# A decoder trunk on one core: the last down projection as seven block products instead of eight

## The reference

```python
def swiglu_ffn(h, w_gu, w_down):
    g, u = jnp.split(h @ w_gu, 2, axis=-1)
    return (jax.nn.silu(g) * u) @ w_down
...
for i in range(DEPTH):                     # DEPTH = 2
    x = x + 0.5 * swiglu_ffn(rmsnorm(x, n_ffn1[i]), ffn1_w_gu[i], ffn1_w_down[i])
    ...                                    # token mixer, cross attention
    x = x + 0.5 * swiglu_ffn(rmsnorm(x, n_ffn2[i]), ffn2_w_gu[i], ffn2_w_down[i])
return rmsnorm(x, n_final)
```

## Time and profile before

| | us |
|---|---|
| median of 3 runs | 1934.61 |
| lowest, highest | 1934.22, 1935.02 |
| the profiled execution, whole time | 1933.99 |
| its span in the trace | 1932.2 |
| PE busy | 1923.7 |
| DVE busy | 1347.7 |
| ACT busy | 964.4 |
| POOL busy | 329.0 |

### The profile page before, as it was taken

The page is one execution under the profiler, slowest core; times in us unless marked ns, Lnnn a source line. Parts: engine busy times, 40 slices in busy tenths (PEclk is TensorE's granted clock), DMA queues, the critical chain, the costliest instruction groups (busy, mean ns, idle before and its releaser), DMA issues.

```text
span 1932.2 us, 31908 instructions
## 1 busy us (share of the span) xinstructions
PE 1923.7 (100%) x12020; PEld 1740.5 (90%) x12020; DVE 1347.7 (70%) x2111; ACT 964.4 (50%) x1612; POOL 329.0 (17%) x331
## 2 busy tenths in 40 slices
PE   9999999999999999999999999999999999999998
PEld 7998998888898889989998998999898889989997
DVE  7865875687765658847866985687487569837854
ACT  7542554355554546524544653365356446524543
POOL 2200212100112121101201120121312123401200
PEclk9999999999999999999999999999999999999999
DMA  6734974323443627736943683695353427847932
GB/s 181 164 109 117 181 153 138 109 67 108 131 128 114 173 87 171 157 103 150 186 111 119 135 169 98 140 189 132 110 179 121 109 70 180 173 153 164 188 109 87
DMA packets 385097, 263.82 MB, mean 137 GB/s; under 512 B 19314, under 2 KB 367600, under 8 KB 384992
## 3 DMA queue, kind: packets, MB, share of 16 engines
q1 hardware_dynamic: 303840, 209.22, 36.4%
q0 software_dynamic: 72224, 51.19, 17.3%
q10 hardware_dynamic: 8928, 2.11, 0.5%
HBM read 251.99 MB, written 10.49 MB: 136 GB/s over the span
## 4 chain that ended last, share of the span: by engine, by line
PE 97%; DVE 1%; issue 1%; ACT 1%; DMA 0%; ACTq 0%
PE ps L434 19%; PE ps L435 18%; PE ps L436 18%; PE ps L1068 14%; PE ps L1067 14%; PE ps L1066 14%; DVE w_lo L2118 0%; ACT w_hi L1447 0%; PE ps L992 0%; PE ps L926 0%; DVE sums L2876 0%; DMA x_tok<-in_x 0%; DVE sums L2896 0%; DVE up L3065 0%; PE ps L1192 0%
## 5 line engine op out<-in xcount | busy, mean ns | idle before, releaser
L2118 DVE TENSOR_TENSOR w_lo<-raw,w_hi 128x512 fp32r<-128x512 f32 (+5 forms) x367 | 397.1, 1096 | 299.7 <-ACT w_hi L1447 299.3
L1447 ACT ACTIVATE w_hi<-raw 128x512 fp32r<-128x512 f32 (+5 forms) x367 | 342.6, 951 | 298.5 <-PE ps L436 255.1
L1067 PE MATMUL ps<-s_lo,w_hi 128*128 128x256 f32 x1248 | 353.2, 283 | 0.0
L1068 PE MATMUL ps<-s_hi,w_lo 128*128 128x256 f32 x1248 | 353.2, 283 | 0.0
L1066 PE MATMUL ps<-s_hi,w_hi 128*128 128x256 f32 x1248 | 353.2, 283 | 0.0
L1068 PE MATMUL ps<-h_hi,w_lo 128*128 128x256 f32 x936 | 264.9, 283 | 0.0
L1067 PE MATMUL ps<-h_lo,w_hi 128*128 128x256 f32 x936 | 264.9, 283 | 0.0
L1066 PE MATMUL ps<-h_hi,w_hi 128*128 128x256 f32 x936 | 264.8, 283 | 0.0
L1066 PEld LDWEIGHTS ps<-s_hi,w_hi 128*128 128x128 f32 x1248 | 239.6, 192 | 0.0
L1067 PEld LDWEIGHTS ps<-s_lo,w_hi 128*128 128x128 f32 x1248 | 239.6, 192 | 0.0
L1068 PEld LDWEIGHTS ps<-s_hi,w_lo 128*128 128x128 f32 x1248 | 239.6, 192 | 0.0
(11 more groups left out here) (406 smaller groups left out, 3789.8 us busy)
## 6 DMA issues: line engine op xcount, KB each, us to landing
raw<-in_ffn_w_gu SPq DMA_DIRECT2D x110, 512.0 KB, 5.0
raw<-in_ffn_w_down SPq DMA_DIRECT2D x36, 768.0 KB, 4.4
outer_even<-in_ffn_w_gu SPq DMA_DIRECT2D x70, 256.0 KB, 3.2
outer_even<-in_ffn_w_gu POOLq DMA_DIRECT2D x70, 256.0 KB, 5.4
raw<-in_ffn_w_gu SPq DMA_DIRECT2D x64, 256.0 KB, 6.1
raw<-in_x_w_kv SPq DMA_DIRECT2D x16, 1024.0 KB, 6.1
raw<-in_ffn_w_down SPq DMA_DIRECT2D x24, 640.0 KB, 4.2
outer_odd<-in_ffn_w_gu SPq DMA_DIRECT2D x54, 256.0 KB, 3.6
```

Of the source, the lines that this page charges most:

```text
L1067: nc.tensor.matmul(to, hi[:, kk, :], right_lo, start=False, stop=False, skip_group_check=True)
L1068: last = nc.tensor.matmul(to, lo[:, kk, :], right_hi, start=False, stop=kk == KH - 1, skip_group_check=True)
L1447: return nc.scalar.activation(out_ap, in_ap, ACT.Copy, **kw)
L2118: return nc.vector.tensor_tensor(out_ap, value, hi.bitcast(F32), ALU.subtract)
```

## The change

The last block's gate and up slots go in one run (`RUNS = (2, 2, 2, 1)`): two plain slots, then twenty mixed ones, then the whole down projection. The gated values stay in fp32 (`mid`, 22 pieces of 128 by 512) and are not split when they are made. Hidden pieces 0 to 10 and 11 to 21 are the two halves of the inner dimension, tokens 0 to 255 and 256 to 511 two halves of the rows, and output columns 0 to 511 and 512 to 1023 two halves of the columns. On these blocks the down projection is seven products in the order P1, P2, P5, P6, P3, P7, P4, each over 11 pieces and two token tiles. A product is cut in six tiles (five of two pieces, one of one), 42 tiles in all, numbered k. For each tile ACT and DVE split the weights (ring of four tiles) and the left operand (ring of eight tiles; the first two have places of their own), the latter four tiles ahead.

Sums of weights for P5, P6 and P4 are made in `w_chain`, by an addition in a DMA from POOL (P5), by DVE (`chain_second_sum`, P6) and by another DMA addition (P4); P7's are made by DMA additions onto P3's. `w_chain` starts for its first eight pieces as a copy that ACT makes of P1's weights (x_scaled_ready counts it), and SP loads P2's weights into `raw` only after that copy. Sums of the gated values are made in place by DVE (`second_form`, `fourth_form`, `third_form`, and an addition in each mixed slot from the twelfth hidden piece on). Each product is added to `x_by_token` with its signs (`take_product`). In the mixed run the splitting of the gated values (`half_mid_hi`, `half_mid_lo`) is gone. `turn_x` is as it was, but the load of `final_gain` is moved behind the run, and the additions for slots 10 to 19 now follow the two loads of `x` in POOL's order.

The core of the diff (the waits are cut where the text above tells them):

```diff
+    RUNS = (2, 2, 2, 1)
+    DOWN_ORDER = (P1, P2, P5, P6, P3, P7, P4)
+    DOWN_TILES = ((0, 2), (2, 2), (4, 2), (6, 2), (8, 2), (10, 1))
+    POSTS = {P1: ((0, 0, 1), (1, 0, 1)), P2: ((0, 0, -1), (1, 0, -1)), P5: ((2, 1, 1), (3, 1, 1)),
+             P6: ((0, 1, -1), (1, 1, -1)), P3: ((0, 1, 1), (1, 1, 1)),
+             P7: ((2, 1, -1), (3, 1, -1), (2, 0, 1), (3, 0, 1)), P4: ((2, 0, -1), (3, 0, -1))}
...
+            def load_down_products():
...
+                for g in range(2):
+                    sp.wait_ge(sig.w_lo_ready, SLOTS + tile(P1, 2 * g + 1) + 1)
+                    sp.wait_ge(sig.x_scaled_ready, CHAIN_COPIED + g + 1)
+                    load_rows(P2, g)
...
-                pool.dma_start(final_gain[:], io.n_final.unsqueeze(0).broadcast_to([P, D])).then_inc(sig.gain_loaded, 16)
...
+            def add_down_sums():
+                down = io.ffn2_w_down[1].rearrange("(k p) n -> p k n", p=P)
...
+                for g, (k0, nrows) in enumerate(DOWN_GROUPS):
...
+                    pool.dma_start(w_chain[:, k0:k0 + nrows, :], down[:, k0:k0 + nrows, SEQ:], accum_op=ALU.add)\
+                        .then_inc(CHAIN_ADDED[g][0], 16)
+                for g, (k0, nrows) in enumerate(DOWN_GROUPS):
+                    pool.wait_ge(sig.w_lo_ready, SLOTS + tile(P6, 2 * g + 1) + 1)
...
+                    pool.dma_start(w_chain[:, k0:k0 + nrows, :], down[:, HALF + k0:HALF + k0 + nrows, 0:SEQ],
+                                   accum_op=ALU.add).then_inc(CHAIN_ADDED[g][0], 16)
+                for g, (k0, nrows) in enumerate(DOWN_GROUPS):
+                    pool.wait_ge(sig.w_lo_ready, SLOTS + tile(P3, 2 * g + 1) + 1)
+                    pool.dma_start(rows_of(P3, g), down[:, k0:k0 + nrows, SEQ:], accum_op=ALU.add)\
+                        .then_inc(T3_ADDED[g][0], 16)
...
             turn_x()
-            add_run(3, 1)
+            for l in range(C + 2, mixed_count(3, 0)):
+                add_outer(3, 0, l)
+            add_down_sums()
...
+            def down_products():                      # PE
+                for k in range(LAST_TILE):
+                    i, q = DOWN_ORDER[k // PER], k % PER
+                    pe.wait_ge(sig.form_lo_ready, FORMS_DONE + k + 1)
+                    pe.wait_ge(sig.w_lo_ready, SLOTS + k + 1)
...
+                    for j in range(2):
+                        to, ts = ps[:, DOWN_BANK[i][j], :], slice(j * P, (j + 1) * P)
+                        for n in range(nrows):
...                                                    # three matmuls of 512 columns
...
+            def down_products():                      # ACT
+                copied = {4: 0, 5: 1}
+                nc.scalar.activation(idle[:], eps[:], ACT.Sqrt)
+                down_hi(3)
+                for k in range(LAST_TILE):
+                    if k in copied:
...
+                        hi_part(w_chain[:, k0:k0 + nrows, :], rows_of(P1, g)).then_inc(sig.x_scaled_ready, 1)
+                    if k >= 4:
+                        down_hi(k)                     # waits for PE's tile k - 4
+                    if k + 4 < LAST_TILE:
+                        down_form_hi(k + 4)
...
+            def down_products():                      # DVE
...
+                for k in range(LAST_TILE):
+                    if k >= 4:
+                        down_lo(k)
+                    if k + 4 < LAST_TILE:
+                        down_form_lo(k + 4)
+                    if tile(P5, 0) <= k + 4 < tile(P5, 0) + PER:
+                        second_form(k + 4 - tile(P5, 0))
+                    if tile(P5, 1) <= k < tile(P5, 1) + PER:
+                        chain_second_sum(k - tile(P5, 1))
+                    if tile(P6, 1) <= k < tile(P6, 1) + PER:
+                        fourth_form(k - tile(P6, 1))
+                    if tile(P3, 1) <= k < tile(P3, 1) + PER:
+                        third_form(k - tile(P3, 1))
+                    if k % PER == 3 and k > PER:
+                        take_product(DOWN_ORDER[k // PER - 1])
+                    if k == 19:
+                        early_gained(0)
...
+                early_gained(1)
+                for tt in (2, 3):
+                    take_product(P4, (tt,))
+                    late_gained(tt)
+                    late_scaled(tt)
```

More of the change, by code:

```diff
@@ L109, in place_ffn @@
             if n == 3:
[L110 to L116, removed]
+                return
             for pair in range(C // 2):
@@ L195, in sum_count, with tile, down_out @@
         return OPENED + 3 * m - transfers_before(m) + step - int(by_transfer(m))
+    def tile(i, q):
+        return PER * DOWN_ORDER.index(i) + q
+    def down_out(n, part):
+        return OUTS if n == 3 else at["down", n, part, 0, 0].out
     def first_of_run(m):
@@ L493, in mixed_banks, with evacuated_after, early, token_half @@
+        def evacuated_after(i):
+            return OUTS + sum(len(POSTS[p]) for p in DOWN_ORDER[:DOWN_ORDER.index(i) + 1])
+        def early(tt):
+            return int(tt >= 2)
+        def token_half(tt, half):
+            return x_by_token[:, tt, half * SEQ:(half + 1) * SEQ]
         def mixed_banks(n, part):
-            o = at["down", n, part, 0, 0].out
+            o = down_out(n, part)
             return ((o + 2) % 4, o % 4), (o + 1) % 4
@@ L1170, in ffn @@
                     if n == 3:
[L1171 removed]
+                        down_products()
                     else:
@@ new lines, in token_out @@
+            def token_out(tt):
+                act.wait_ge(sig.tok_ready, len(TOK_FEEDS) + tt + 3)
+                act.wait_ge(sig.y_gained, tt + 1 + 2 * (tt // 2))
+                ready = token_half(tt, early(tt))
+                nc.scalar.activation(ready, ready, ACT.Copy, scale=y_rms[:, tt:tt + 1]).then_inc(sig.y_out_by_act, 1)
+                act.wait_ge(sig.y_out_by_act, tt + 1)
+                first = early(tt) * SEQ
+                act.dma_start(out[0].rearrange("(t p) d -> p t d", p=P)[:, tt, first:first + SEQ], ready)\
+                    .then_inc(stored, 16)
@@ L2224, in mixed_run, with taken, gated @@
                 banks, d = mixed_banks(n, part)
-                turning = (n, part) == (3, 0)
+                turning = n == 3
+                def taken(m, s, step):
+                    if m >= mixed_first[n, part] + 2:
+                        dve.wait_ge(sig.mixed_dve_step, dve_step(m - 2, step))
+                    else:
+                        dve.wait_ge(sig.evacuated, at["gu", 3, s - 2].out + 2)
+                def gated(to, gate, value, s):
+                    if s < HALF:
+                        return nc.vector.tensor_tensor(to, gate, value, ALU.mult)
+                    return nc.vector.scalar_tensor_tensor(to, gate, -1.0, value, ALU.mult, ALU.mult)
                 def seed_fourth(m, s, b):
```

467 lines of the change are left out of this document (326 added, 141 removed).

## The result

| | before | after |
|---|---|---|
| median, us | 1934.61 (5 runs) | 1945.53 (5 runs) |
| lowest, highest | 1934.20, 1935.44 | 1943.77, 1946.28 |
| the profiled execution; its span | 1933.99; 1932.2 | 1945.88; 1944.2 |

The change makes the kernel slower: ratio 1.0055, 95% interval 1.0041 to 1.0069, 10.9 us. The forecast was 1936.0 with a range of 1929 to 1947. The time is in the range, but the likeliest case (no change within 0.2%) was not what happened.

What follows compares the result with a forecast made beforehand. PE, busy 1923.7 of 1932.2 us, was taken as the bound. -15.0 saved + 5.5 (term 1) + 8.9 (term 2) + 1.9 (term 3) = +1.3 us, giving a median of 1936.0 us, range 1929 to 1947.

Steps and rivals of the forecast that it cites:

- the likeliest case: Whole kernel: measured time the same as before within 0.2% (3.9 us), chance 0.44.
- PE as the bound, and what is saved: Last block: PE has no gap, so 66 fewer down projection matmuls at 0.2267 us save 15.0 us.
- Term 1: Slot 10: its additions, issued behind the loads of x, land late and hold up PE, 5.5 us (0 to 9).
- Term 2: Down phase: DVE no longer free and rows late, 8.9 us (3.4 to 26).
- the start: Down phase: copy done at 9.3, P2's first rows at 15.7, split at 17.9; PE is there at 14.96.
- DVE's work: Down phase up to P3's last tile: 58.9 us of DVE work from 17.9 ends at 76.8; PE waits 3.4 us.
- the waits for rows: Down phase: P2's second and third rows each some 2.4 us late, P5's last addition 1 us; counted 5.5 us.
- Term 3: Kernel's end: token tile 3 waits behind tile 2's chain on DVE, 1.9 us (1 to 3).
- The additions become the bound: Rival: P4's and P7's DMA additions in one queue make PE stand at P7's start, 1945 to 1953 us; chance 0.17.
- Transfers on time: Rival: loads and additions quicker than mid-bounds, term 1 at 3 and term 2 at 4.6, 1929.1 us; chance 0.18.
- ACT's waits: Down phase, a sign to show the forecast: ACT waits on w_chain; no size given.

Runs made afterwards that it cites:

- e1: Slot 10's two additions issued by POOL ahead of the loads of x, against the changed kernel: 1940.82 us.
- e6: DVE's six sums for P6's weights cut to 128 elements, against the changed kernel: 1942.86 us.
- e2: P5's three additions wait until P2's rows have landed, against the changed kernel: 1937.92 us.
- e3: P5's three additions cut to one 128 x 128 block each, waits left as they are, against the changed kernel: 1933.87 us.
- e7: e1, e2, e4 and a reordered end (both last token tiles added before either is scaled) in one kernel, against the changed kernel: 1930.41 us.
- e11: e7 with SP reloading P1's rows instead of ACT's copies, P5's additions behind P2's last rows, loads of P3's rows and the rest behind those additions: 1934.51 us.
- e12: e7, copies kept, with P5's additions all behind P2's last rows and SP's loads of P3's rows and the rest behind those additions: 1937.09 us.
- e8: e7 with SP's loads of P3's rows and of the rest waiting for P5's additions: 1930.66 us.
- e4: ACT's two copies of chain rows made four tiles earlier, against the changed kernel: 1944.00 us.

## Why the prediction was right in places and wrong in size

**PE as the bound, and what is saved.** Right: 66 matmuls of 0.2267 us fewer, and each wait shows in full.

**Term 1 (5.5 us).** 5.2 by the trace, 4.7 by e1. The addition was issued at 1693.40 (said: 1694.0), and DVE had it at 1703.4 rather than 1705.5; the 1.4 us to land in that sum stand in no row. PE stood 3.7 us, 1.8 less than forecast; 1.5 at the lower clock, which the forecast had not, brought it back. The mechanism was right, its sum partly by luck.

**Term 2 (8.9 us), the start.** The copy was to be done at 9.3 us behind the first tile (1812.86) and was at 9.7; P2's first rows at 15.7, and ACT had them at 15.6. The 3 us until P2 starts came as 1.2 at P1's fifth tile and 1.9 at P2's first.

**Term 2, DVE's work (3.4 us with the start).** Full from P5 on, as said (above 98% to 1920). The 3.4 us held the start's 2.9; measured are 3.1 and then 2.4 (e6), 2 more.

**Term 2, the waits for rows (5.5 us): the step that failed.** It is "By this queue P2's second rows land at about 21 and its third at 29". They were there at 26.5 and 37.9. The rate of additions was not at fault: 183 GB/s was taken, and alone they ran at some 200. Nor was the total: the last of P5's additions, issued at 1827.3, landed 23.1 us later, at 37.6, before my 43. I treated all transfers as one line, in which what is issued first is done first. In fact two lines take turns by packets, and the packets of additions are the longer ones, so P2's rows paid for additions that nobody needed yet. And the one line was not even carried through for the third rows. What was issued before them (SP's two loads, the load of the rest, POOL's three additions):

```profile
1822.61 3.64 SPq L614 DMA_DIRECT2D raw<-in_ffn_w_down  x2
1826.34 0.80 SPq L630 DMA_DIRECT2D w_rest<-in_ffn_w_down  x1
1832.51 11.98 SPq L614 DMA_DIRECT2D raw<-in_ffn_w_down  x2
...
1822.83 1.26 POOL L889 DMA_DIRECT2D w_chain<-in_ffn_w_down  x1 [8.94 <-ACT w_chain L1564]
1826.10 2.55 POOL L889 DMA_DIRECT2D w_chain<-in_ffn_w_down  x2 [2.01 <-ACT w_chain L1564]
```

With the forecast's rates, 366 and 183 GB/s, all of it in one line from 9.3 us on puts the second rows at 21 and the third at an estimated 35; 29 comes out only without the rest and the third addition. So of the 9 us by which the third rows were later than forecast, some 6 are transfers left out of the line and 3 the turns. (Two smaller slips: 2.4, 2.4 and 1 make 5.8 and not 5.5, and SP's loads in that window are 5.8 MB, not 5.5.) Together this is 13.0 us with the clock, 9 without, instead of 5.5 (of which P5's 1 did not come); e2 and e3 show it. The Trainium skill, "DMA: Bandwidth & Descriptors", section "Queues, rings and completion order", says that each DMA engine goes round the queues that have work, at packet granularity; the trace agrees (800 and 799 packets). Before the change no large addition ran beside a large load, but one line of the view of the earlier trace rows bore on it, and I did not take it up. SP's load of 512 KB, issued at 1698.01 beside the loads of x, took 7.5 us to land, where 768 KB had taken 4.4:

```profile
raw<-in_ffn_w_down SPq DMA_DIRECT2D x1, 512.0 KB, 7.5
```

**The clock.** 5.5 us of the surplus are matmuls at a granted 1.2 GHz behind three gaps of 3.4 to 5.2 us. PE had no gap in the block before, so no row showed it, and the forecast had no term for it.

**Term 3 (1.9 us).** 1.9. Right.

**Not seen:** 1.0 us in the last gate and up slot, where DVE splits the down projection's first tile ahead of `high_up`, whose bank PE wants. It is in all thirteen traces of the change. That moving the split cures it was not tried.

**The rivals.** "The additions become the bound" gave 1945 to 1953 and so has the time, but not the cause: it put the loss at P7's start, and PE is busy for 30.00 of the 30 us there, with additions of 1 MB landing in 8.3 to 9.3 us. That the range reached to 1947 rests on these additions, which cost nothing, so that the time lies in it is in part luck. "Transfers on time", 1929.1, is near what e7 gets with the order mended. ACT's waits were to be on `w_chain`; they were on `raw`, and came to `w_chain` only where P5's additions were moved back, as in e2.

## What to carry to other kernels

A transfer that is not needed yet, on another queue, takes half of the packets from the one that is needed now. Place it by when its bytes are needed: order it behind the urgent loads by a wait on their landing (7.6 us here), but don't chain everything: loads held back until an addition had landed came too late for the next consumer (e11, e12). When you forecast a landing, write down every transfer issued before it, on all queues. And price a gap in a dense matmul stream at more than its length: here 12.6 us of gaps in three places carried 5.5 us of slow matmuls behind them.

## What the runs showed of the hardware

- Accumulating DMAs with rows of 2 KB ran at some 200 GB/s alone (189 to 214 in most slices), about half of a plain load's 410. Their packets took 0.169 us against 0.094 beside each other.
- Beside each other, additions and loads moved 262 GB/s in all, 131 each. Plain transfers from POOL and SP together moved 386. In both cases the queues took turns packet for packet, whether POOL's packets held 2 KB (800 to 799) or 4 KB (258 to 267).
- The turns did not begin at once: from 1828 to 1830 us POOL's queue moved 171 packets and SP's 2, though SP's second load had been issued at 1825.9. Why is open.
- Behind all gaps of PE of 3.2 us and more the granted clock fell from 1.0 to 0.5 for some microseconds (1.5 to 2.3 us lost each in the kernel after, 1.3 to 2.7 over all experiments). Shorter ones went both ways: after a gap of 2.76 us the surplus was 3.0 us in e7, so nothing was lost, and 4.5 in e8; after one of 2.29 us in e2 nothing, after one of 2.21 in e4, 12 us behind an earlier gap, 1.6, and after one of 2.68 in e1, 11 us behind an earlier one, 1.7. The length of the gap alone does not tell.
